# Attention cycle of a hybrid GLA / GQA / MoE layer: probability transposes joined in groups of eight, and the value products in one run of eight key blocks and one of two

## What is computed

```
def block_attention(q, k, v):            # 8 query heads, 2 key/value heads, head size 64
    def one(qblk):                        # 128 queries
        s = einsum('bqkgd,bskd->bkgqs', qblk, k) * scale
        p = softmax(s, axis=-1)
        return einsum('bkgqs,bskd->bqkgd', p, v)
    o = lax.map(one, qb)                  # 8 blocks of 128 latent queries
# latent queries: keys = 1024 rotated latent keys + 256 cached context keys
```

## Time and profile before

| | |
|---|---|
| median of 3 runs | 2782.96 us (2781.19 to 2786.1) |
| the profiled execution, its own time | 2780.45 us |
| its span, first to last instruction | 2778.8 us |
| PE busy | 2464.0 us, 89% of the span |
| PE weight loads | 1360.0 us, 49% |
| DVE busy | 1621.5 us, 58% |
| ACT busy | 1321.6 us, 48% |
| POOL busy | 816.8 us, 29% |

### The profile page before, as it was taken

One profiled execution on the slowest core, in us unless ns is written; L12 is line 12 of the kernel. 1 busy time (PEld: TensorE's weight loads), 2 busy tenths in 40 slices (PEclk: granted clock), 3 DMA queues, 4 the chain that ended last, 5 costly groups with the idle time before them and its releaser, 6 DMA issues. The chain is left out here.

```text
span 2778.8 us, 55870 instructions
## 1 busy us (share of the span) xinstructions
PE 2464.0 (89%) x19085; PEld 1360.0 (49%) x19086; DVE 1621.5 (58%) x1909; ACT 1321.6 (48%) x1351; POOL 816.8 (29%) x853
## 2 busy tenths in 40 slices
PE   4999987899999957989999999789998999999992
PEld 0555444566664533545445554345544455544551
DVE  0222226467773654793581676999778735166895
ACT  0111116245441223782571666888668625165781
POOL 3121221300002323432332444333343333233432
PEclk8999997999999978989999999899999999999996
DMA  8000008230004227895493687999979936158984
GB/s 333 28 9 17 17 0 281 70 103 0 0 0 154 91 97 263 287 340 183 148 387 93 223 283 246 384 397 394 366 228 383 369 104 212 30 155 290 358 304 145
DMA packets 176502, 539.95 MB, mean 194 GB/s; under 512 B 20644, under 2 KB 36438, under 8 KB 175380
## 3 DMA queue, kind: packets, MB, share of 16 engines
q1 hardware_dynamic: 146240, 488.92, 47.2%
q0 software_dynamic: 26720, 46.85, 8.0%
q10 hardware_dynamic: 3496, 3.61, 0.4%
HBM read 494.69 MB, written 45.21 MB: 194 GB/s over the span
## 5 line engine op out<-in xcount | busy, mean ns | idle before, releaser
L1916 PE MATMUL psum<-arena 128*64 128x512 bf16 x12528 | 1437.2, 386 | 94.6 <-DVE arena L1811 89.1
L1916 PEld LDWEIGHTS psum<-arena 128*64 128x64 bf16 x12528 | 728.3, 112 | 750.6 <-DVE arena L1811 111.6
L1811 DVE TENSOR_TENSOR arena<-arena 128x2048 bf16<-128x2048 f32 x384 | 858.0, 2285 | 178.9 <-ACT arena L1713 153.4
L1713 ACT ACTIVATE arena<-arena 128x2048 bf16<-128x2048 f32 x384 | 706.4, 1898 | 42.2 <-PE psum L1916 20.0
L1666 POOL DMA_INDIRECT expert_sums<-arena x90 | 187.1, 2079 | 535.1 <-issue 514.9
L558 PE MATMUL psum<-arena 128*128 128x512 f32 (+2 forms) x864 | 304.5, 509 | 1.2 <-issue 1.2
L1646 POOL DMA_INDIRECT arena<-expert_inputs,arena x88 | 139.0, 1580 | 493.4 <-DMA arena<-expert_lists 427.7
L558 PEld LDWEIGHTS psum<-arena 128*128 128x128 f32 x864 | 151.7, 192 | 132.3 <-issue 128.9
L1815 DVE TENSOR_TENSOR arena<-psum,arena 128x512 bf16<-128x512 f32 x87 | 59.7, 686 | 212.2 <-ACT arena L1723 212.2
L1734 ACT ACTIVATE arena<-psum,arena 128x512 f32<-128x512 f32 x87 | 59.6, 685 | 205.1 <-PE psum L1916 149.3
L1719 ACT ACTIVATE arena<-psum 128x1024 bf16<-128x1024 bf16 x87 | 88.4, 1017 | 122.2 <-PE psum L1916 118.2
(11 more groups left out here) (246 smaller groups left out, 2233.5 us busy)
## 6 DMA issues: line engine op xcount, KB each, us to landing
arena<-in_w_gu SPq DMA_DIRECT2D x256, 1024.0 KB
arena<-in_w_down SPq DMA_DIRECT2D x128, 1024.0 KB, 6.7
arena<-in_w_ada SPq DMA_DIRECT2D x12, 2048.0 KB, 11.8
arena<-in_w_in SPq DMA_DIRECT2D x8, 1168.0 KB, 20.4
arena<-in_x_sample SPq DMA_DIRECT2D x16, 512.0 KB
arena<-mod_rows SPq DMA_DIRECT2D x12, 512.0 KB, 6.2
expert_sums<-arena SPq DMA_DIRECT2D x10, 512.0 KB, 6.5
expert_inputs<-arena SPq DMA_DIRECT2D x10, 512.0 KB, 2.8
```

The source lines that it names most:

```text
L1713: nc.scalar.activation(w_hi[c], raw[c], ACT.Copy).then_inc(sem(f"hi_made{c}"), 1)
L1811: nc.vector.tensor_tensor(w_lo[c], raw[c], w_hi[c], ALU.subtract).then_inc(sem(f"lo_made{c}"), 1)
L1916: last = nc.tensor.matmul(bank(b)[group(g)], parts[part][:, cols], w[:, kk, g * H:(g + 1) * H], start=False, stop=(k == KT - 1 and part == 1))
```

## The change

Only PE's stream in the attention stage changes. In a cycle, group 1 moves ahead of the scores, so that groups 0 and 1 stand together. Groups 2 and 3 follow the scores directly. The products over key blocks 0 to 7, which stood in three pieces between the groups, come in one run behind group 3. Group 4 and the last two key blocks stay where they were. The wait values are the same; each wait goes with what it protects. The number of matmuls, transposes and copies is unchanged.

```
--- before.py
+++ after.py
@@ -1217,28 +1217,24 @@
                         if r == 1:
                             wait(pe, sem("share_kept"), t + 1)
                         turn(0)
+                        wait(pe, sem("exp_made"), n * 2)
+                        if not early:
+                            wait(pe, sem("pT_dve"), m * 3)
+                        turn(1)
                     if scores_on(t):
                         wait(pe, sem("exp_made"), n * 2)
                         score(n, r)
                     if turns_on(t, r):
-                        wait(pe, sem("exp_made"), n * 2)
-                        if not early:
-                            wait(pe, sem("pT_dve"), m * 3)
-                        turn(1)
+                        wait(pe, sem("pT_act"), m * 2 + 1)
+                        turn(2)
+                        wait(pe, sem("pT_act"), m * 2 + 2)
+                        turn(3)
                     if mixes_on(t, r):
                         wait(pe, sem("pT_act"), m * 2)
                         wait(pe, sem("pT_dve"), m * 3)
                         if r == 2:
                             wait(pe, sem("norm_done"), t + 1)
-                    mix(0, 3)
-                    if turns_on(t, r):
-                        wait(pe, sem("pT_act"), m * 2 + 1)
-                        turn(2)
-                    mix(3, 6)
-                    if turns_on(t, r):
-                        wait(pe, sem("pT_act"), m * 2 + 2)
-                        turn(3)
-                    mix(6, 8)
+                    mix(0, 8)
                     if turns_on(t, r):
                         wait(pe, sem("pT_dve"), m * 3 + 1)
                         turn(4)
```

## The result

| | before | changed |
|---|---|---|
| median of 18 runs each | 2782.83 us (2777.4 to 2788.02) | 2788.73 us (2785.24 to 2793.09) |
| ratio, with its 95% interval | | 1.0021 [1.0013, 1.0028] |
| span of the profiled execution | 2778.8 us | 2785.6 us |

The changed kernel is slower, by 0.21%. The interval excludes no change, but reaches to both sides of the 0.2% line. The forecast was 2788.8 us.

What follows compares the result with a forecast made beforehand. PE's own pace was taken to bound the attention stage; 4.4 (plain cycles) + 0.1 (cycles with the spread) + 1.6 (first cycles) - 0.3 (last cycles) = +5.8 us, so 2788.8 us, with an 8-in-10 range of 2783 to 2796.

Steps and rivals of the forecast that it cites:

- The bound before, and the entry price: Attention stage: PE's own pace sets the 8.08 us cycle of ten segments; each segment entry costs about 0.15 us.
- the rule that the prediction weighed: Trainium skill's statement that PE's queue pulls weight loads ahead of running matmuls; by it entries would be free, same sum.
- Group 4 released at E + 3.68: With E the end of the scores, DVE's copy of group 2 lets PE start group 4 3.68 us later.
- The slack of 0.29: Before the change, group 4 started at 3.97 us behind the scores' end though allowed at 3.68: 0.29 us.
- Period 8.23: Plain attention cycle, scores to scores: 8.23 us against 8.08, +0.15 each, +4.4 us over 29 periods.
- Group 1's waits at nothing: Waits between joined groups 0 and 1 ahead of the scores cost 0; the other bound was 0.15 us a cycle.
- The margin of 0.18: DVE's copy of the last group 4 is done only 0.18 us before group 1 is due.
- The first cycles, +1.6: Stage start: group 4 0.8 us later, partly at half clock, plus 0.8 for group 1's wait on group 4's copy.
- The last cycles, -0.3: Cycle 31's group 4 comes 0.3 us earlier with no scores following; in cycle 32 waits about equal saved entries.
- Kept entries without the wait: Rival: DVE's copy doesn't hold group 4, four entries saved each cycle, 17.4 us, giving 2765.6 us; chance 0.05.
- Open waits: Rival: group 1's waits aren't hidden, up to 0.15 us a cycle more, +4.4, giving 2793.2 us; chance 0.14.
- Clock: Rival: new PE idle time drops the clock, one slow score group in four cycles, about 18 us: 2806; chance 0.05.

Runs made afterwards that it cites:

- E3: Changed kernel with PE's order kept, but the copy of group 2 made by ACT ahead of its exponentials instead of by DVE: 2768.1 us, ratio 0.9945.
- E4: Kernel before, with group 1 joined to group 2 behind the scores and group 4 joined to the next group 0, copies unmoved: 2768.34 us, ratio 0.9946.
- E2: Kernel before with only group 1 moved ahead of the scores, products still in pieces between the groups: 2787.88 us, ratio 1.0019.
- E6: Changed kernel with DVE copying group 2 between the two maxima instead of behind both: 2785.86 us, ratio 1.0014.
- E7: Changed kernel profiled once more, nothing edited, a single run: 2786.16 us.
- E8: Kernel before the change profiled once more, nothing edited, a single run: 2778.82 us.
- E1: Changed kernel with group 1 put back behind the scores, long run of products kept: 2778.1 us, ratio 0.9986.
- E5: E4's order with E3's copies; in cycles with the spread of shares, six key blocks before group 4 and four behind the spread: 2762.97 us, ratio 0.9932.

## Why the prediction was right

Point by point, by its own steps.

**The bound before, and the entry price.** Right. E3 and E4 reach 7.47 us, which is 8.08 less four entries, with different orders of PE and different copies; what they share is the number of segments. So the entries are not free here, as they would be by the rule that the prediction weighed.

**Group 4 released at E + 3.68.** Right, to 0.01: 3.68 in the changed kernel and in E2. It was read from a wait of the first cycle, the only place where the profile before showed what follows a copy of DVE that PE waits for. The slack of 0.29 before was in no list of waits; it was the difference of two starts. E3 left PE's order as it was and took this wait away by giving the copy to ACT, and the kernel became 20 us faster than the changed one. E3 takes work from DVE as well; but E6, with all copies on DVE, also brings group 4 back to its own pace, and E4 gains as much as E3 with no copy moved. That this wait held the cycle is shown.

**Period 8.23.** Right. For the 28 periods from the scores of cycle 3 on the forecast has 28 x 0.15 + 0.1 = 4.3; measured were 4.47. The cycles with the spread take 9.46 or 9.47 us against 9.28, 0.03 more than the 0.15 of a plain cycle, where the forecast had put 0.01 more.

**Group 1's waits at nothing.** Right: the joined groups took 1.02 or 1.03, in the loop too (1.05 or 1.06 in five of E7's). The margin of 0.18 held.

**The first cycles, +1.6.** Too much, for the reason that the forecast took the half-clock stretch of the one profile as given: it put 0.8 where the four transposes cost 0.44 at full clock. Up to the scores of cycle 2 it is 9.00 us in E7 against 7.71 in E8, +1.29, and the period behind it, the 29th of the sum, adds 0.03 in place of 0.15. In the profiles here a half-clock stretch lay over the first cycle (the first of the kernel before, E1, E3, E4, E5), over the second (the first of the changed kernel), over both (E6), or over neither (E2, E7, E8).

**The last cycles, -0.3.** Measured -0.37.

**Rivals.** Kept entries without the wait: E3 shows what it would have been, and that it needed another engine for the copy. Open waits: no. Clock: 1.00 through all the plain cycles, with 0.69 us of idle time in each. In two profiles half clock was granted in the second cycle: the first of the changed kernel, after the wait of 2.47 us, and E6, after waits of 0.97 and 1.54 us. It was not in E2 and E7, which have the same 2.47 us, nor in either profile of the kernel before. Whether the longer wait makes such a stretch more likely isn't settled by so few executions.

**The time itself.** The sum gave +5.8, the medians of 18 runs differ by 5.9, and the stage measures +5.5 in the pair E7 and E8 (from the first group 0 to the last run of products, 269.22 against 263.74 us) and +4.5 in the first pair. That the total came out to 0.1 us is luck: the interval of the ratio alone is 4 us wide, and in the pair at full clock the first cycles were put 0.4 us too high and the other periods 0.2 too low.

## What to carry to other kernels

Where an engine is busy all the time, look for the releases that arrive just before they are needed: the slack is the start of the waiting step less the end of the copy or transfer plus its signal, and no view of waits lists it. Reordering that saves time ahead of such a release saves nothing, and what it puts behind the release is paid in full; the same saving behind the release, or with the release moved to an engine that has time for it, is kept. Here six segments a cycle gave +0.2% in one order (the change), -0.1% in a second (E1) and -0.5% in a third (E4).

## What the runs showed of the hardware

A switch between fp32 transposes of 128 x 128 and fp32 matmuls (scores or products) cost PE about 0.15 us at full clock, whether a semaphore wait lay at the switch or not: ten segments a cycle took 8.08 us and six took 7.47. Between the spread and the products behind it, both matmuls, no such price shows (sixteen records in 0.97 us, E5). Waits inside a run of transposes cost next to nothing when they were already fulfilled (1.02 or 1.03 us for eight in nearly all cycles, 1.07 at most). Transposes follow the granted clock: four took 569.33 - 568.31 = 1.02 us at 1.2 GHz and 568.36 - 567.80 = 0.56 at 2.4 GHz (E8). Where a group on PE waited for a copy, it started 0.05 or 0.06 us behind the end of the copy's record.
